# A fused two-block transformer kernel: the slots of the two rings of split weights, 4160 bytes apart in place of 4096

## The chip, the cores and the metric

The kernel runs on one core of a Trainium2 chip. The core has five engines that work side by side: TensorE (PE, matmuls; its weight loads are listed as PEld), VectorE (DVE), ScalarE (ACT), GpSimd (POOL) and SyncE (SP), which here only issues transfers. They share the on-chip memory SBUF, with 128 partitions; matmuls write to the eight banks of PSUM. The metric is the device time of one execution in microseconds, as a median of several runs.

## The reference

The input x is [1, 512, 1024] in float32. A first block applies a mixer (half of its channels by a stabilised mLSTM in chunks, half by gated linear attention, both forward and backward) and a convolutional gated network; a second block of two layers applies a pooling and convolution mixer or a latent attention, cross attention to a memory of 256 rows, and again a gated network. Each part is preceded by an RMS norm. Cut to its frame:

```python
def first_block(x, ...):
    x = x + rms_norm(hybrid_mixer(rms_norm(x, g0), w_in, ..., w_out), g1)
    x = x + rms_norm(conv_ffn(rms_norm(x, g2), w_gate, w_up, conv_w, conv_b, w_down), g3)
    return x

def second_block(x, mem, ...):
    for l in range(2):
        h = rmsnorm(x, norm_mix_g[l])
        x = x + (pool_conv_mixer(h, ...) if l == 0 else mla_attention(h, ...))
        x = x + memory_cross_attention(rmsnorm(x, ...), rmsnorm(mem, ...), wq, wkv, wo)
        x = x + conv_ffn_2(rmsnorm(x, ...), w_up, conv_w, conv_b, w_down)
    return rmsnorm(x, final_norm_g)
```

Nearly all of the arithmetic is products of activations with weight matrices, in float32.

## The kernel before

Activations lie transposed in SBUF: 128 channels on the partitions, 512 positions along a row, eight such tiles for 1024 channels. The weights were laid out in units of 128 partitions by up to 1024 numbers (4096 bytes in each partition). Unit u goes to slot u % 4 (RING is 4) of three rings. SyncE loads it into `raw`. Then it is split into two numbers of a shorter format, high and low: GpSimd writes wH = raw + 0 (L637) and, once that is done, wL = raw - wH (L640). For 40 units (a_o, b_r and the memory's weights) ScalarE writes the high part (L1583) and GpSimd the low part only (L695 and L707). Activations are split in the same way, into hnH and hnL or actH and actL.

TensorE makes each product out of three matmuls (L750 to L752): high by high, low by high and high by low. A ring tile is either the weight operand (128x128 at a time) or the moving one (up to 512 columns). A unit with all 512 positions is 8 x 3 = 24 matmuls of 512 columns. When a unit's last matmul is done, `unit_done` rises; GpSimd waits for it before it writes the slot again, and TensorE waits for `split` before it reads the next unit. SyncE waits for `split` before it loads raw again. The order of all this is written out in the program; nothing in it looks at an address.

The helper `at` gives each tensor the next free address in a partition, rounded up to 64 bytes. By it raw begins at 100544, wH at 116928 and wL at 133312, each ring 16384 bytes long, followed by the vectors VT, the constants CT, MASK, zero, rstd, rcol, ssq, sq, lnb, lncol and onesR, then a reserved gap of 1536 bytes and tmpY. Earlier are XT at 1472, hnH at 17856, hnL at 34240, actH at 50624, actL at 67008 and MIX at 83392. The line numbers of the changed kernel are one higher from L38 on.

The prediction also speaks of L680 (GpSimd, low part of an activation out of MIX and hnH), L736 (GpSimd, MIX by rstd over the last 256 positions), L2263 and L2869 (VectorE, low parts of activations and of the memory's keys and values).

Of the kernel before, what the change touches and what calls it, by code (L numbers as in the profile page):

```python
# [17 lines left out]
F32R = mybir.dt.float32r  # L18
I32 = mybir.dt.int32
ALU = mybir.AluOpType  # L20
ACT = mybir.ActivationFunctionType
AX = mybir.AxisListType

P = 128
# [10 lines left out]
ENDS = (slice(0, 256), slice(256, 512))  # L35
RING = 4
UNIT = 1024
BIG = 1e30  # L38
HALVES = (1, 2, 4, 8, 16, 32, 64)
POOL_WINDOWS = (2, 4, 8, 16)  # L40
# [235 lines left out]
def program(nc, x_t, mem_t, positions, weights, pool_w, gla_w2, vecs, consts, masks, out):  # L276
    ctx = ExitStack()
    with ctx:
        place = [1472]

        def at(name, shape, dt=F32, offset=None):

            size = int(np.prod(shape[1:])) * 4
            if offset is None:
                offset = place[0]
                place[0] += (size + 63) // 64 * 64
            return nc.alloc_sbuf_tensor_at(name, shape, dt, offset=offset)

        def sem(name):
            return ctx.enter_context(nc.semaphore(name))  # L290
# [10 lines left out]
        MIX = at("MIX", [P, KD, S])  # L301
        place[0] += 768
        raw = at("raw", [P, RING, UNIT])
        wH = at("wH", [P, RING, UNIT], F32R)
        wL = at("wL", [P, RING, UNIT], F32R)
        VT = at("VT", [P, NVEC])
        CT = at("CT", [P, NCONST])
        neg_at = place[0]
# [9 lines left out]
        lnb = at("lnb", [P, S])  # L318
        lncol = at("lncol", [P, NB])
        onesR = at("onesR", [P, P], F32R)  # L320
        place[0] += 3 * 512
        tmpY = at("tmpY", [P, 1])
        scr = place[0]
        TOP = 229344
# [146 lines left out]
        def sig(name):  # L471

            if name not in named:
                named[name] = sem(name)
            return named[name]
# [15 lines left out]
        def psum(n):  # L491
            return bank[BANK[n]]
# [1039 lines left out]
        def _(act):  # L1532
            step, nsq = [0], [0]
            run = nc.scalar.activation
# [43 lines left out]
            def memory_high(i):  # L1578

                u = MEMORY[i]  # L1580
                act.wait_ge(loaded[u % RING], 16 * (u // RING + 1))
                act.wait_ge(unit_done, u - RING + 1)
                run(wH[:, u % RING, :], raw[:, u % RING, :], ACT.Copy).then_inc(sig("memory_hi"), 1)  # L1583

            def memory_input(l):

# [131 lines left out]
            for i in range(9):  # L1718
                if i < 8:
                    decay(i)  # L1720
                if i == 0:
                    first_values()
                if 1 <= i <= 4:
                    log_gate(i - 1)
                elif i > 4:
                    if i == 5:
                        first_fade(3)
                    if i == 8:
                        memory_high(0)
                        memory_high(1)  # L1730
                    n = TILE0["b_v"] + i - 5
                    tile_wait(act, n)
                    free(run(VB[:, i - 5, :], psum(n)[:, :], ACT.Copy, scale=rcol[:, i - 5:i - 4]), n)
# [31 lines left out]
            for cc in range(2):  # L1765
                for lev in range(1, 10):
                    if 2 <= lev <= 7:
                        key_mix(cc, lev)
                    if cc == 0 and lev in (4, 6, 8) or (cc, lev) == (1, 2):
                        memory_high(4 + (lev // 2 - 2 if cc == 0 else 3))  # L1770
                    if cc == 0 and lev in (2, 3):
                        memory_high(lev)
                        if lev == 3:
                            act.wait_ge(sig("y_sums"), 8)
                        for h in (2 * lev - 4, 2 * lev - 3):
                            gone_wait(act, TILE0[f"nd{2 * h + 1}"])
                            gone_wait(act, TILE0[f"nd{2 * h + 1}"] + 1)
                            for b in range(NB):
                                run(sq[:, h % 2, b * P:b * P + P], Y[:, b, h, :], ACT.Square, accum_out=ysq[:, 4 * h + b:4 * h + b + 1])\
                                    .then_inc(sig("y_sums"), 1)  # L1780
                    if cc == 0 and lev == 4:
                        act.wait_ge(sig("y_sums"), 16)
                        link(run(yln[:, :], ysq[:, :], ACT.Ln, bias=v("eps"), scale=1.0 / P))
                        link(run(yrt[:, :], yln[:, :], ACT.Exp, scale=-0.5))
                    if cc == 0 and 5 <= lev <= 8:
                        h = lev - 5
                        for b in range(NB):
                            run(Y[:, b, h, :], Y[:, b, h, :], ACT.Copy, scale=yrt[:, 4 * h + b:4 * h + b + 1])\
                                .then_inc(sig("y_scaled"), 1)
                    if cc == 1 and lev in (3, 5, 7, 9):  # L1790
                        h = (lev - 3) // 2
                        act.wait_ge(sig("head_out"), h + 1)
                        run(actH[:, h, :], psum(TILE0["y_turn"] + h)[:, :], ACT.Copy).then_inc(sig("y_hi"), 1)
                    if cc == 1 and lev in (2, 4):
                        head_square(lev // 2 - 1)
# [435 lines left out]
        def _(dve):  # L2231
# [814 lines left out]
            def att_max(h):  # L3046

                for t, b, c0, o in SCORE_AT:
                    n = TILE0["score"] + 3 * h + t
                    if o != 2:  # L3050
                        tile_wait(dve, n)
                    w = (b + 1) * P
                    own = psum(n)[:, c0 * P:c0 * P + w]
                    last = nc.vector.tensor_tensor_reduce(own, own, not_past[:, S - w:], -scale, BIG, ALU.add, ALU.min,
                                                          mst[:, h % 2, o:o + 1])
# [29 lines left out]


# [1 line left out]
def columns(a):  # L3088

# [20 lines left out]
def lay_weights(a):  # L3110
# [38 lines left out]
    for i, (gate, up, down) in enumerate(layers):  # L3149
        pairs = np.stack([stationary(gate), stationary(up)], axis=1).reshape(2 * NF, P, D)  # L3150
        at = 0
        for t, c in enumerate(THIRDS):
            groups[f"ff{i}_gu{t}"] = pairs[2 * at:2 * (at + c)]
            groups[f"ff{i}_d{t}"] = stationary(down[at * P:(at + c) * P])
            at += c
    laid = np.zeros((NUNITS, P, UNIT), np.float32)
    for name, count, width in UNITS:
# [34 lines left out]
def constants():  # L3192
# [4 lines left out]
    def put(name, w):  # L3197
        laid[:, CONST[name]:CONST[name] + w.shape[1]] = w
    put("ident", (p == f) * 1.0)
    put("ones", np.ones((P, P)))  # L3200
    put("past", (f < p) * BIG)
    put("future", (f > p) * BIG)
    put("upto", (p <= f) * 1.0)
    put("since", (p >= f) * 1.0)
    put("twice", (p == f) * 2.0)
    put("neg_future", (f > p) * -BIG)
    counts = [np.minimum(np.arange(16) + 1, w).astype(np.float32) for w in POOL_WINDOWS]
# [28 lines left out]
```

## Time and profile before

| | us |
|---|---|
| median of 3 runs (2006.04 to 2006.3) | 2006.12 |
| the profiled execution | 2006.59 |
| its span in the trace | 2004.8 |
| TensorE busy in it | 1981.7 (99%) |
| GpSimd busy | 1448.1 (72%) |
| VectorE busy | 971.0 (48%) |
| ScalarE busy | 616.6 (31%) |

The span is the time between the first and the last recorded instruction. Matmuls are pipelined: one of 512 columns is recorded as some 390 ns long, while the next starts after 227 ns or so; the starts tell the rate. The granted clock of TensorE was 0.998 of full speed in the mean of the core.

### The profile page before, as it was taken

Reading aid. Unit: us, or ns where it says so; the run is one execution under the profiler, and the core shown is the slowest. Engines: PE = TensorE matmul, PEld = TensorE weight load, DVE = VectorE, ACT = ScalarE, POOL = GpSimd, SP = SyncE. Lnnn points to the kernel's source line nnn. Section 1 sums busy time; section 2 is a strip of 40 time slices with the busy share of each in tenths; the row PEclk is TensorE's granted clock in tenths of the full one; section 3 lists DMA queues with packets and bytes.
Section 4 is the critical chain, followed back from the end, with each engine's and each line's share of the span. In section 5 each row is a group of like instructions: output and inputs, shape, how many; then the busy total and the mean of one; then the engine's idle time right before and its main releaser. Section 6 shows DMA issues by size and latency. Waiting matters only on the chain.

```text
span 2004.8 us, 25752 instructions
## 1 busy us (share of the span) xinstructions
PE 1981.7 (99%) x9476; PEld 1625.3 (81%) x9476; DVE 971.0 (48%) x1607; ACT 616.6 (31%) x1172; POOL 1448.1 (72%) x736
## 2 busy tenths in 40 slices
PE   8999989999999999999999999999999999999998
PEld 6788778888888888888888888877678888888887
DVE  5566444233433899565431332364656554223134
ACT  5454452221013435433210110136743331011012
POOL 7623379777877877974977778687569398777774
PEclk9999999999999999999999999999999999999999
DMA  4741233222323345321332223234013123222322
GB/s 166 145 66 64 76 109 116 94 95 95 96 91 108 106 145 170 109 81 53 109 102 95 94 94 102 72 101 123 2 33 109 49 95 105 95 95 96 102 84 66
DMA packets 58299, 190.79 MB, mean 95 GB/s; under 512 B 6416, under 2 KB 10256, under 8 KB 58096
## 3 DMA queue, kind: packets, MB, share of 16 engines
q1 hardware_dynamic: 54720, 184.42, 29.9%
q10 hardware_dynamic: 3472, 4.88, 0.8%
q8 instruction: 76, 1.25, 0.3%
q14 instruction: 31, 0.25, 0.0%
HBM read 183.50 MB, written 2.10 MB: 93 GB/s over the span
## 4 chain that ended last, share of the span: by engine, by line
PE 96%; POOL 1%; ACT 1%; DVE 1%; DMA 1%; SPq 0%; issue 0%; DVEq 0%; POOLq 0%
PE bank L750 29%; PE bank L751 29%; PE bank L752 29%; PE bank L1458 2%; PE bank L1135 1%; PE bank L1472 1%; PE bank L1488 1%; PE bank L1046 1%; DMA raw<-weights 1%; POOL wL L640 0%; POOL wH L637 0%; PE bank L1208 0%; PE bank L1157 0%; PE bank L990 0%; SPq L585 0%; PE bank L1149 0%
## 5 line engine op out<-in xcount | busy, mean ns | idle before, releaser
L637 POOL TENSOR_TENSOR wH<-raw,zero 128x1024 fp32r<-128x1024 f32 (+1 forms) x303 | 579.5, 1912 | 376.5 <-PE bank L752 358.9
L640 POOL TENSOR_TENSOR wL<-raw,wH 128x1024 fp32r<-128x1024 f32 (+1 forms) x303 | 719.6, 2375 | 23.8
L750 PE MATMUL bank<-hnH,wH 128*128 128x512 f32 (+1 forms) x1456 | 571.5, 392 | 14.4 <-POOL wL L631 8.0
L751 PE MATMUL bank<-hnL,wH 128*128 128x512 f32 (+1 forms) x1456 | 568.5, 390 | 0.0
L752 PE MATMUL bank<-hnH,wL 128*128 128x512 f32 (+1 forms) x1456 | 568.1, 390 | 0.0
L750 PEld LDWEIGHTS bank<-hnH,wH 128*128 128x128 f32 (+1 forms) x1456 | 273.4, 188 | 77.2 <-issue 8.2
L752 PEld LDWEIGHTS bank<-hnH,wL 128*128 128x128 f32 (+1 forms) x1456 | 273.6, 188 | 58.6 <-issue 0.7
L751 PEld LDWEIGHTS bank<-hnL,wH 128*128 128x128 f32 (+1 forms) x1456 | 273.7, 188 | 56.4 <-issue 0.2
L750 PE MATMUL bank<-actH,wH 128*128 128x512 f32 (+1 forms) x802 | 309.4, 386 | 0.0
L752 PE MATMUL bank<-actH,wL 128*128 128x512 f32 (+1 forms) x802 | 308.2, 384 | 0.0
L751 PE MATMUL bank<-actL,wH 128*128 128x512 f32 (+1 forms) x770 | 295.7, 384 | 0.0
L2371 DVE TENSOR_TENSOR bank<-bank,rstd 128x512 f32<-128x512 f32 x66 | 46.1, 699 | 283.1 <-PE bank L752 283.1
L752 PEld LDWEIGHTS bank<-actH,wL 128*128 128x128 f32 x802 | 150.7, 188 | 30.1
L750 PEld LDWEIGHTS bank<-actH,wH 128*128 128x128 f32 x802 | 150.7, 188 | 30.1 <-issue 0.2
L751 PEld LDWEIGHTS bank<-actL,wH 128*128 128x128 f32 x770 | 144.7, 188 | 28.7 <-issue 0.2
L1602 ACT ACTIVATE bank<-gpad,VT 128x512 f32<-128x512 f32 x66 | 51.7, 783 | 345.0 <-DVE gpad L2369 345.0
L1605 ACT ACTIVATE cva<-bank 128x512 f32<-128x512 f32 x66 | 39.5, 599 | 369.1 <-DVE bank L2295 369.1
L707 POOL TENSOR_TENSOR wL<-raw,wH 128x1024 fp32r<-128x1024 f32 x32 | 76.6, 2404 | 30.6 <-ACT wH L1583 30.3
L2398 DVE TENSOR_TENSOR XT<-bank,XT 128x512 f32<-128x512 f32 x32 | 22.1, 692 | 135.3 <-PE bank L752 135.3
L2758 DVE SCALAR_TENSOR_TENSOR bank<-glp,VT,bank 128x512 f32<-128x512 f32 x120 | 81.9, 747 | 0.1
L1553 ACT ACTIVATE hnH<-XT,VT 128x512 fp32r<-128x512 f32 x48 | 34.6, 721 | 131.2 <-DVE XT L2845 106.4
L2369 DVE TENSOR_TENSOR gpad<-bank,rstd 128x512 f32<-128x512 f32 x66 | 45.7, 692 | 56.9 <-PE bank L752 56.8
(418 smaller groups left out, 2580.1 us busy)
## 6 DMA issues: line engine op xcount, KB each, us to landing
raw<-weights SPq DMA_DIRECT2D x315, 512.0 KB, 3.5
raw<-weights SPq DMA_DIRECT2D x28, 384.0 KB, 3.0
XT<-x_t SPq DMA_DIRECT2D x8, 256.0 KB, 6.5
XT<-x_t ACTq DMA_DIRECT2D x1, 2048.0 KB, 8.5
maxB<-rowM SPq DMA_DIRECT2D x7, 256.0 KB, 16.6
out<-MIX SPq DMA_DIRECT2D x13, 128.0 KB, 1.9
qkO<-qkA SPq DMA_DIRECT2D x4, 256.0 KB, 4.1
memT<-mem_t ACTq DMA_DIRECT2D x1, 1024.0 KB, 5.4
```

The lines of the kernel that those rows point to most:

```text
L637: nc.gpsimd.tensor_tensor(wH[:, slot, 0:w], raw[:, slot, 0:w], nothing.broadcast_to([P, w]), ALU.add)\
L640: nc.gpsimd.tensor_tensor(wL[:, slot, 0:w], raw[:, slot, 0:w], wH[:, slot, 0:w].bitcast(F32), ALU.subtract).then_inc(split, 1)
L707: nc.gpsimd.tensor_tensor(wL[:, slot, 0:w], raw[:, slot, 0:w], wH[:, slot, 0:w].bitcast(F32), ALU.subtract).then_inc(split, 1)
L750: mm(out_, aH, bH, start=first, stop=False)
L751: mm(out_, aH, bL, start=False, stop=False)
L752: return mm(out_, aL, bH, start=False, stop=last)
L1458: last = mm(psum(n)[:, c0 * P:c0 * P + w], QC[0:96, h, b * P:b * P + P], KC[0:96, h, 0:w], start=True, stop=True)
L1602: run(psum(n)[:, :], gpad[:, s_, mid:mid + S], ACT.Identity, bias=v(f"fconv_b{f}", q), scale=v(f"fconv_w{f}", 3 * q + 1)).then_inc(sig("co ...
L1605: free(run(cva[:, s_, :], psum(n)[:, :], ACT.Gelu_apprx_tanh if f == 0 else ACT.Silu), n)
L2369: tt(gpad[:, s_, 2:2 + S], psum(n)[:, :], rstd[:, :], ALU.mult).then_inc(sig("gate_in"), 1)
L2371: tt(psum(n + 1)[:, :], psum(n + 1)[:, :], rstd[:, :], ALU.mult)
L2758: ins = stt(psum(n)[:, :], glp[:, c_, k:k + S], w, psum(n)[:, :], ALU.mult, ALU.add)
```

## The change

The two rings wH and wL get slots of 1040 numbers (4160 bytes), of which the first 1024 are used as before. Each ring becomes 256 bytes longer. The reserved gap behind onesR becomes 512 bytes shorter, so that all that lies behind it keeps its address; what lies between wL and the gap moves by 512 bytes, and wL itself by 256. The ring raw keeps its slots of 4096 bytes. ScalarE's high part, which wrote a whole slot, now names the first 1024 numbers of it. No instruction is added, taken away or moved on any engine, and none has another shape.

```diff
 RING = 4
 UNIT = 1024
+SLOT = UNIT + 16
...
         raw = at("raw", [P, RING, UNIT])
-        wH = at("wH", [P, RING, UNIT], F32R)
-        wL = at("wL", [P, RING, UNIT], F32R)
+        wH = at("wH", [P, RING, SLOT], F32R)
+        wL = at("wL", [P, RING, SLOT], F32R)
...
         onesR = at("onesR", [P, P], F32R)
-        place[0] += 3 * 512
+        place[0] += 1024
         tmpY = at("tmpY", [P, 1])
...
-                run(wH[:, u % RING, :], raw[:, u % RING, :], ACT.Copy).then_inc(sig("memory_hi"), 1)
+                run(wH[:, u % RING, 0:UNIT], raw[:, u % RING, :], ACT.Copy).then_inc(sig("memory_hi"), 1)
```

## Rows read from the trace of the kernel before

**Rows 1.** The page, part 1: busy us (share of the span) xinstructions.

```profile
PE 1981.7 (99%) x9476; PEld 1625.3 (81%) x9476; DVE 971.0 (48%) x1607; ACT 616.6 (31%) x1172; POOL 1448.1 (72%) x736
```

**Rows 2.** The page, part 4: the chain that ended last, by engine.

```profile
PE 96%; POOL 1%; ACT 1%; DVE 1%; DMA 1%; SPq 0%; issue 0%; DVEq 0%; POOLq 0%
```

**Rows 3.** Timeline of 1099 to 1108 us: start us, us, engine line op [idle before].

```profile
1099.32 1.90 POOL L637 TENSOR_TENSOR wH<-raw,zero 128x1024 fp32r<-128x1024 f32 x1 [1.07 <-PE bank L752]
...
1099.66 0.39 PE L750 MATMUL bank<-hnH,wH 128*128 128x512 f32 x1
...
1104.66 1.89 POOL L637 TENSOR_TENSOR wH<-raw,zero 128x1024 fp32r<-128x1024 f32 x1 [0.98 <-PE bank L752]
...
1107.82 0.39 PE L750 MATMUL bank<-hnH,wH 128*128 128x512 f32 x1
```

**Rows 4.** Busy time by stretch: us, then each engine's, granted clock, DMA share, GB/s.

```profile
1000.00:1200.00 200.00, 200.00 (x884) 165.62 (x883) 62.82 (x90) 25.76 (x39) 154.78 (x74) 1.00 0.29 95
```

**Rows 5.** Waits of PE: engine line waited for, us in total, times, longest.

```profile
PE bank L750 <- POOL wL L631: 8.0, 1, 8.0
PE bank L750 <- DVE hnL L2263: 5.6, 1, 5.6
...
PE bank L750 <- POOL wL L640: 0.7, 3, 0.3
```

**Rows 6.** The chain in order of time, 0 to 75 us: start us, us, what.

```profile
13.54 1.90 POOL wH L637
...
15.51 2.42 POOL wL L640
...
57.53 2.72 POOL wL L640
60.25 2.30 POOL wH L637
...
66.96 2.37 POOL wL L640
```

**Rows 7.** Groups of POOL by form: line engine op names shapes xcount, busy, mean ns.

```profile
L640 POOL TENSOR_TENSOR wL<-raw,wH 128x1024 fp32r<-128x1024 f32 x275 | 667.5, 2427 | 21.6
L637 POOL TENSOR_TENSOR wH<-raw,zero 128x1024 fp32r<-128x1024 f32 x275 | 537.4, 1954 | 335.2 <-PE bank L752 317.6 <-DMA raw<-weights 17.4
...
L680 POOL TENSOR_TENSOR hnL<-MIX,hnH 128x512 fp32r<-128x512 f32 x4 | 5.2, 1294 | 9.4 <-ACT XT L1871 9.4
L736 POOL TENSOR_TENSOR MIX<-MIX,rstd 128x256 f32<-128x256 f32 x2 | 1.4, 726 | 14.8 <-ACT rstd L2224 14.8
```

**Rows 8.** Timeline of POOL, 1310 to 1352 us.

```profile
1325.64 2.73 POOL L640 TENSOR_TENSOR wL<-raw,wH 128x1024 fp32r<-128x1024 f32 x1
1335.73 1.89 POOL L637 TENSOR_TENSOR wH<-raw,zero 128x1024 fp32r<-128x1024 f32 x1 [7.36 <-PE bank L752]
...
1344.40 2.34 POOL L637 TENSOR_TENSOR wH<-raw,zero 128x1024 fp32r<-128x1024 f32 x1
```

**Rows 9.** The page, part 5: the first and last of the six largest matmul groups.

```profile
L750 PE MATMUL bank<-hnH,wH 128*128 128x512 f32 (+1 forms) x1456 | 571.5, 392 | 14.4 <-POOL wL L631 8.0
...
L751 PE MATMUL bank<-actL,wH 128*128 128x512 f32 (+1 forms) x770 | 295.7, 384 | 0.0
```

**Rows 10.** Timelines of PE near 777 and near 872 us (matmuls of 256 columns).

```profile
777.22 0.28 PE L750 MATMUL bank<-memH,wH 128*128 128x256 f32 x1
...
777.94 0.28 PE L750 MATMUL bank<-memH,wH 128*128 128x256 f32 x1
...
871.51 0.28 PE L751 MATMUL bank<-KL,qH 128*128 128x256 f32 x1
...
872.23 0.28 PE L751 MATMUL bank<-KL,qH 128*128 128x256 f32 x1
```

**Rows 11.** The line L2869: duration ns min/median/max, first and last start us.

```profile
L2869 DVE TENSOR_TENSOR VL<-VM,actH x8: 680/1878/1978, 880.2 to 1583.5; 128x512 fp32r<-128x512 f32 x8
```

**Rows 12.** Busy time by stretch, behind PE's idle time at 274 us.

```profile
280.20:286.90 6.70, 6.63 (x19) 5.30 (x20) 6.35 (x11) 5.29 (x11) 2.58 (x2) 0.64 0.23 78
```

## The prediction

> **What bounds the kernel now.** I read the page's busy times first: the reader is to see TensorE (PE) busy in 1981.7 of 2004.8 us, 99%, against 72% for GpSimd (POOL) and less for the others [rows 1]. Only a change that makes PE's work shorter, or that keeps PE waiting, can be seen in the time. The chain that ended last says the same by engine, 96% PE, 1% each for POOL, ACT, DVE and DMA [rows 2]. So there are two places where an address in the rings could matter: the rate at which PE reads the split weights, and the POOL passes that write them, where those stand on the chain.
>
> PE's rate is read from the timeline in a steady stretch of the gated network. From the start at 1099.66 to the start at 1107.82 lie 36 matmuls of 128x512, so one starts each 8.16/36 = 0.2267 us [rows 3]. In 1000 to 1200 us there are 884 matmuls in 200 us, 0.2262 us each, with PE busy in all of it [rows 4]; meanwhile POOL was busy for 155 us with reading and writing the rings. A clash between POOL and PE that came and went with POOL's passes would spread these starts; the average leaves no room for it. At 2.4 GHz, the granted clock of the stretch (1.00), 512 columns are 213.3 ns, so 13.3 ns are added to each.
>
> Where PE waited for POOL is in the list of waits: 8.0 us once, at the first unit, and 0.7 us in three later waits [rows 5]. POOL stands on the chain in 13.5 to 17.9 us and in 55.6 to 69.3 us, which is one pair of passes (high part L637, low part L640) and then three more, four pairs in all [rows 6]. Elsewhere a pair costs 1.90 + 2.43 us [rows 3, 7], its high parts start 5.34 us apart (1099.32 and 1104.66), and PE needs 24 x 0.2267 = 5.44 us for a unit [rows 3]: POOL has about 1 us to spare per unit and waits for PE.
>
> **The change part by part.** The instructions are the same, in the same order on every engine, with the same shapes; only addresses differ.
>
> 1. The slots of wH and wL go from 4096 to 4160 bytes apart, and wL starts 256 bytes later. Before, slot s of raw, wH and wL lie exactly 16384 bytes apart, so a pass reads and writes at the same position modulo 4096 (the allocations in the code: 100544, 116928, 133312). After, raw and wH of slot s differ by 64 s more, raw and wL by 256 + 64 s more. What POOL pays for equal positions is read by comparison. Two inputs of 128x256: L736 reads MIX and rstd, whose addresses are 2880 and 832 bytes apart modulo 4096 (c_ = 0 and 1), and takes 726 ns. The two-input pass over equal positions, 128x512 at L680 (MIX is 65536 bytes behind hnH), takes 1294 ns, and 128x1024 at L640 2427 ns [rows 7]. If position cost nothing these must lie on one line: 726 + (2427 - 726)/3 = 1293 ns. They do. So the step is priced at 0 ns per pass. Bounds, below: L640 gets as quick as L637, which reads one full tensor and a broadcast column, 2427 - 1954 = 473 ns less, four times on the chain, -1.9 us. Above: the slowest usual forms of both passes in this trace, 2.73 us for L640 and 2.34 us for L637 [rows 8], against some 2.40 (2.37 and 2.42 in rows 6) and 1.89. On the chain that is 0.33 us on three L640 (the one at 57.53 is at 2.72 already) and 0.45 us on three L637 (the one at 60.25 is at 2.30 already): 1.0 + 1.35 = +2.3 us. I take 0, since the comparison is of the same kind of instruction.
>
> The Trainium skill's GPSIMD Engine Reference, section 2.1, says that the two inputs of such a pass share one physical read port and cannot do better than about 2.5 cycles an element. An estimate from that page at its 1.2 GHz is 2.13 us for 1024 elements; if the present 2.43 us fell to it, four passes would give back 1.2 us. Nothing in that rule depends on the address, and by it too the time stays within what can be told apart.
>
> 2. PE reads wH and wL as weights and as moving operand at new addresses. The page's six largest matmul groups on them are 3 x 1456 + 2 x 802 + 770 = 6742 instructions [rows 9], so 0.6 ns on each would be 4.0 us, 0.2%. Do the 13.3 ns come from the rings' addresses? The comparison is at 256 columns (106.7 ns at 2.4 GHz). Cross attention's matmuls on KL, qH, actH and actL, none in a ring, start 6 in 0.72 us (871.51 to 872.23), 120 ns each; those of the memory values, whose moving operand is in the rings, 6 in 0.72 us (777.22 to 777.94), 120 ns as well [rows 10]. Both have 13.3 ns added. So the addition belongs to the matmul, not the ring, and I take 0. Below, the bound would be all 13.3 ns; the matmuls without a ring exclude it as well as they can. Above, no slower spacing at full clock is tied to an address by any row, and 0 is the nearest.
>
> 3. ScalarE's high parts of 40 units (a_o, b_r and the memory's weights) write a slot cut to UNIT. It is the same 128x1024; nothing is added.
>
> 4. The tables and small tensors between wL and tmpY (VT, CT, MASK, rstd, ssq, sq, lnb, onesR) move by 512 bytes; a reserved gap shrinks by as much, so tmpY and all behind it stay. These are read by DVE and ACT. DVE's two-input subtraction shows what sets its time: VL<-VM,actH takes 680 ns at the least and 1878 in the median [rows 11]. Its two inputs always start a multiple of 1024 bytes apart, with other multiples in the first layer than in the second; the instances near 1.9 us are those beside a POOL pass. Cost 0, unless POOL's phase changes: should POOL's passes shift, DVE's long instances shift with them. PE's largest wait on DVE is 5.6 us, at hnL [rows 5], and there the input is a PSUM bank; a shift has little to bite on.
>
> The Trainium skill's page SBUF — State Buffer, section "Who interferes with whom", has one rule, that only the port pair of VectorE and GpSimd is contended and PE and ACT never wait on anyone. The long DVE instances agree. By that rule a new spacing can neither slow nor speed PE, and the sum is the same 0.
>
> Sum: the profiled execution took 2006.59 us, 2004.8 of span and 1.8 around it; with 0 from all four steps it would be the same again. It stands 0.47 us above the runs' median of 2006.12, and against that median the forecast is 2006.1.
>
> **The rivals.**
> A. Equal positions do cost POOL its second read, and the spacing frees it. For it: L640 is 473 ns longer than L637. Against: the straight line through the three two-input passes. Time: -1.9, 2004.2 us. That is still within 0.2%, because only four pairs are on the chain.
>
> B. PE's 13.3 ns come, in part or whole, from where the weights lie relative to the moving tensors. For it: they are 6% of nearly every matmul. Against: the same 13.3 ns without a ring. In whole, 6742 x 13.3 ns = 90 us, about 1916; a twentieth of it is 4.5 us, about 2001.6. This is the only way to a clear gain.
>
> C. Slower: odd multiples of 64 bytes cost POOL, and its passes take 2.34 and 2.73 us everywhere. A pair, 5.07 us, plus 0.08 us between passes is still under PE's 5.44, so the steady stretches hide it. It would show where POOL was just in time: the +2.3 us on the chain, and, if PE takes the last of them at once, the three pairs that POOL runs without a break from 1335.73 to about 1349 us [rows 8]: 3 x 0.33 + 2 x 0.45 = +1.9. Together +4.2, 2010.3 us. It decides from a pair about 0.75 us longer; from 1 us longer POOL would be the bound in the steady stretches too. Against: the same straight line, with one operand pair that is not at equal positions.
>
> D. The spacing doesn't act at all, because nothing depends on the position of the slots. That is my forecast, and its sign in the trace is equality of every group.
>
> A fifth matter is the clock: at 280.2 to 286.9 us the granted mean is 0.64 after PE's idle time at 274 to 280, and 19 matmuls take 6.7 us where 19 x 0.2267 = 4.3 would do, a cost of 2.4 us [rows 12]. As no instruction before it changes its duration, I expect it again at the same place; without it the time would be 2.4 us less, 2003.7, just under the range.
>
> **How the numbers follow.** Forecast (D) 0.82, at 2006.1; A 0.06, at 2004.2; B 0.06, of it 0.01 inside 0.2%; C 0.05, all slower; 0.01 is left to matters unnamed and counted as no change. A difference under about 0.2%, 4 us, can't be told from no change. Faster is thus 0.05, slower 0.05, same 0.90. The range takes in the low bound of step 1 (2004.2) and its high bound on the chain (2008.4): 2004.0 to 2008.5.
>
> **What would show it.** Right: means of 2427 ns for L640 and 1954 for L637, the usual L637 at 1.89; 0.2267 us between matmul starts near 1100 us; PE's waits for POOL 8.0 and 0.7 us again; the clock low once, near 280 us. Rival A shows as L640 nearer 1950, B as a spacing below 0.226 or above 0.228, C as L637 near 2.34 us everywhere and PE waiting for POOL beyond 3 us. The forecast is wrong if the time moves by over 4 us, and its reasoning is wrong if a pass or the spacing moves by over 2% even with the time unmoved.

## The result and the profile after

The changed kernel takes 2031.88 us, a median of 4 runs (2030.73 to 2032.16), against 2006.21 us of 4 runs before: a ratio of 1.0125, with a 95% interval of 1.0112 to 1.0137. It is 25.7 us slower. The forecast was no change, with 2008.5 us as the top of the range.

Busy times, the changed kernel's page (part 1), against [rows 1]:

```profile
PE 2007.4 (99%) x9476; PEld 1627.2 (80%) x9476; DVE 978.2 (48%) x1607; ACT 616.2 (30%) x1172; POOL 1449.2 (71%) x736
```

PE is busy 25.7 us longer, the whole loss, with the same 9476 matmuls. DVE grew by 7.2 us and POOL by 1.1 us; ACT fell by 0.4 us. The chain by engine, against [rows 2], has PE at 98% and POOL at 0%:

```profile
PE 98%; ACT 1%; DVE 1%; DMA 0%; SPq 0%; POOL 0%; issue 0%; DVEq 0%; ACTq 0%
```

So PE waits for nobody more than before, which its waits say too (engine, line waited for, us in total, times, longest), against [rows 5]:

```profile
PE bank L751 <- POOL wL L632: 7.5, 1, 7.5
PE bank L751 <- DVE hnL L2264: 5.8, 2, 5.6
...
PE bank L751 <- POOL wL L641: 0.5, 2, 0.3
```

The two GpSimd passes, by form, take 2438 and 1944 ns where [rows 7] had 2427 and 1954:

```profile
L641 POOL TENSOR_TENSOR wL<-raw,wH 128x1024 fp32r<-128x1024 f32 x275 | 670.6, 2438 | 21.6
L638 POOL TENSOR_TENSOR wH<-raw,zero 128x1024 fp32r<-128x1024 f32 x275 | 534.6, 1944 | 355.9 <-PE bank L753 338.5 <-DMA raw<-weights 17.4
```

What changed is the rate of the matmuls. The stretch of [rows 4] holds 870 of them in place of 884, PE again busy in all of it:

```profile
1000.00:1200.00 200.00, 200.00 (x870) 163.16 (x869) 64.47 (x93) 28.29 (x43) 156.55 (x73) 1.00 0.29 96
```

That is 0.2299 us each in place of 0.2262, at the same granted clock of 1.00. (Such a count also takes in the matmuls that the edges of the stretch cut, so it is a little low; the starts are exact.) Over the matmuls of 512 columns that read a ring and are followed by the next start within 300 ns (7361 of 7462), the mean from one start to the next is 230.5 ns, and 227.0 ns before: 3.5 ns x 7361 = 25.8 us.

Which matmuls pay shows when the units are told apart. A unit's slot is known by counting GpSimd's low passes (the m-th fills slot m % 4). In the changed kernel's timeline of PE these are the first matmuls of four units in a row, in slots 0, 1, 2 and 3, and of the next in slot 0:

```profile
1123.50 0.39 PE L751 MATMUL bank<-hnH,wH 128*128 128x512 f32 x1
...
1128.95 0.40 PE L751 MATMUL bank<-hnH,wH 128*128 128x512 f32 x1
...
1134.55 0.39 PE L751 MATMUL bank<-hnH,wH 128*128 128x512 f32 x1
...
1140.12 0.39 PE L751 MATMUL bank<-hnH,wH 128*128 128x512 f32 x1
...
1145.63 0.39 PE L751 MATMUL bank<-hnH,wH 128*128 128x512 f32 x1
```

The 24 matmuls take 5.45 us in slot 0, 5.60 in slot 1, 5.57 in slot 2 and 5.51 in slot 3. Before, each took 5.44. Slot 0 of wH has the address it had, and slot 0 of wL lies 256 bytes later: this costs next to nothing. The slots that lie 64, 128 and 192 bytes further do cost. That POOL's passes were not behind it shows already here: matmuls that start while POOL, DVE and ACT are all idle are 230.5 ns apart as well (some 900 of them).

### The profile page after: what moved, and what is told of

Its sections match the earlier page's. It is cut to its first block, busy times and chain, and to the rows that moved or that the text cites. A ratio compares the mean times of both kernels' runs of the same rounds, so it can differ in the third digit from the quotient of the medians.

```text
span 2030.0 us, 25752 instructions
## 1 busy us (share of the span) xinstructions
PE 2007.4 (99%) x9476; PEld 1627.2 (80%) x9476; DVE 978.2 (48%) x1607; ACT 616.2 (30%) x1172; POOL 1449.2 (71%) x736
## 4 chain that ended last, share of the span: by engine, by line
PE 98%; ACT 1%; DVE 1%; DMA 0%; SPq 0%; POOL 0%; issue 0%; DVEq 0%; ACTq 0%
PE bank L751 30%; PE bank L753 30%; PE bank L752 30%; PE bank L1459 2%; PE bank L1136 1%; PE bank L1473 1%; PE bank L1489 1%; PE bank L1047 1%; DMA raw<-weights 0%; PE bank L1209 0%; PE bank L1158 0%; PE bank L991 0%; SPq L586 0%; PE bank L1150 0%; PE bank L1101 0%; PE bank L1270 0%
```

## The experiments

The theory, R: before, all that PE reads together with a ring slot (hnH, hnL, actH, actL, and behind tmpY the tiles memH, memL, cH, cL and poolL) begins at the same address modulo 256 as every slot, at 192. A matmul is slowed when its weights and its moving operand differ there. The rivals: G, GpSimd's passes at unequal positions clash with PE's reads; A, the absolute address of a weight block counts; S, the spacing of 4096 itself helps; T, the moved tables cost. Experiments 1 to 11 ran once each, experiment 12 ten times, with the kernel before beside them on the same chip: 2007.59 us for experiments 1 to 4 and 2006.13 for 5 to 8, one run each, and a median of 2006.54 over 13 runs for 9 to 12. Those 13 lie between 2005.71 and 2007.82 us, so a single run tells differences of more than about 2 us.

The numbers on slots below are the mean ns from one start to the next in units whose 24 matmuls read hnH, hnL and the rings, in slots 0 to 3 (30 to 38 units each); the last column is the mean over all ring matmuls of 512 columns, taken as above:

| kernel | rings against hn, modulo 256, by slot | slot 0 | 1 | 2 | 3 | all ring matmuls |
|---|---|---|---|---|---|---|
| before | 0 | 226.7 | 226.7 | 226.7 | 226.7 | 227.0 |
| after | 0, 64, 128, 192 | 227.1 | 233.2 | 232.3 | 229.6 | 230.5 |
| 1, tables only | 0 | 226.7 | 226.7 | 226.7 | 226.7 | 227.0 |
| 2, 4352 apart | 0 | 226.7 | 226.7 | 226.7 | 226.7 | 227.0 |
| 3, rings +64 | 64 | 233.3 | 233.3 | 233.3 | 233.3 | 233.1 |
| 4, whole map +64 | 0 | 226.7 | 226.7 | 226.7 | 226.7 | 227.0 |
| 5, activations +64 | 192 | 229.0 | 228.9 | 228.9 | 228.9 | 229.4 |
| 6, 4224 apart | 0, 128, 0, 128 | 227.3 | 232.9 | 227.4 | 232.9 | 230.4 |
| 7, wH alone | wH 0, 64, 128, 192; wL 0 | 227.1 | 233.2 | 232.9 | 230.6 | 230.8 |
| 8, wL alone | wL 0, 64, 128, 192; wH 0 | 226.8 | 230.9 | 231.9 | 231.1 | 230.2 |
| 9, rings +128 | 128 | 233.1 | 233.1 | 233.1 | 233.1 | 232.9 |
| 10, rings +32 | 32 | 233.3 | 233.3 | 233.3 | 233.3 | 233.3 |
| 11, raw -64 | 0 | 226.7 | 226.7 | 226.7 | 226.7 | 227.0 |

**1. The spacing undone, the rest kept.**

```diff
         wH = at("wH", [P, RING, UNIT], F32R)
+        place[0] += 256
         wL = at("wL", [P, RING, UNIT], F32R)
+        place[0] += 256
...
-        place[0] += 3 * 512
+        place[0] += 1024
```

> Slots 4096 apart again; only what came with the spacing stays: wL starts 256 bytes later, VT, CT, rstd and the other small tensors 512 bytes later. Theory R (the matmul's two reads, the running moving operand and the weight load of the next matmul, cost more when their addresses differ modulo 256; in the trace after, ring matmuls start 227.1 ns apart in slot 0, 232 to 233 in slots 1 and 2, 229.5 in slot 3): every address modulo 256 is that of before, so 226.7 ns everywhere and about 2006.2 us. Theory T (the moved tables and wL's base cost the time): about 2032 us.

2007.36 us: T falls. wL's base and the tables' new places cost nothing.

**2. Another spacing that is a multiple of 256.** The edit is one of the changed kernel:

```diff
-SLOT = UNIT + 16
+SLOT = UNIT + 64
...
-        place[0] += 768
+        place[0] += 256
         raw = at("raw", [P, RING, UNIT])
         wH = at("wH", [P, RING, SLOT], F32R)
...
         onesR = at("onesR", [P, P], F32R)
-        place[0] += 1024
```

> Slots of wH and wL 4352 bytes apart, 4096 + 256 (raw begins 512 bytes earlier to make room). Theory R: a multiple of 256, so all slots at 226.7 ns and about 2006.2 us. Theory S (a spacing that is a multiple of 4096 is what helps, any other costs): 2030 us or more. Theory G (GpSimd's passes clash with PE's reads when raw and the rings are not at the same position modulo 4096): about 2030 us.

2007.46 us, and the steady stretch is that of before:

```profile
1000.00:1200.00 200.00, 200.00 (x884) 165.67 (x883) 63.10 (x91) 26.35 (x40) 154.75 (x73) 1.00 0.29 95
```

S falls, and so does G in the form that I gave it: slots at unequal positions modulo 4096 are free as long as they are equal modulo 256.

**3. The old spacing, both rings 64 bytes later.**

```diff
         raw = at("raw", [P, RING, UNIT])
+        place[0] += 64
         wH = at("wH", [P, RING, UNIT], F32R)
         wL = at("wL", [P, RING, UNIT], F32R)
...
         onesR = at("onesR", [P, P], F32R)
-        place[0] += 3 * 512
+        place[0] += 3 * 512 - 64
```

> Slots 4096 apart, but both rings begin 64 bytes later (wH and wL and the small tensors behind them), so that every slot is at the position that slot 1 of wH and wL has after the change (modulo 256). Theory R: every slot like slot 1 there, about 5.7 ns on each of some 7370 ring matmuls of 512 columns, +42 us, 2048 us, spacing near 232.4 ns in all slots. Theory A (the absolute address of the weight block modulo 256 is what counts): the same. Theory S (the spacing is the cause): 2006 us.

2050.34 us, 42.8 above its kernel before: nearly the number of R, with slots 4096 apart. The steady stretch has 859 matmuls:

```profile
1000.00:1200.00 200.00, 200.00 (x859) 161.15 (x858) 64.72 (x93) 27.75 (x42) 155.13 (x73) 1.00 0.30 95
```

The same trace shows a sign that R did not foresee. Matmuls of 256 columns get quicker with their weights 64 bytes above. These two starts in the memory's keys, with the ring as weights, have 42 matmuls from the one to the other:

```profile
791.55 0.28 PE L751 MATMUL bank<-memH,wH 128*128 128x256 f32 x1
...
796.32 0.28 PE L751 MATMUL bank<-memH,wH 128*128 128x256 f32 x1
```

4.77 us are 113.6 ns each, where the same product took 120 in the kernel before [rows 10].

**4. The whole map 64 bytes later.**

```diff
-        place = [1472]
+        place = [1536]
```

> Slots 4096 apart and the whole map of SBUF 64 bytes later, activations and rings alike. Theory R (only the difference of the two addresses counts): 226.7 ns and 2006.2 us. Theory A (the absolute address of the weight block, or of any operand, modulo 256 counts): near 232 ns and 2048 us.

2005.43 us and 884 matmuls: A falls. The weights have the absolute addresses of experiment 3, but the activations moved along, and the loss is gone.

```profile
1000.00:1200.00 200.00, 200.00 (x884) 165.62 (x883) 62.11 (x89) 25.76 (x39) 155.40 (x73) 1.00 0.29 95
```

**5. The activations moved and the rings left.**

```diff
+        place[0] += 64
         hn_at = place[0]
...
-        place[0] += 768
+        place[0] += 704
```

> Slots 4096 apart and the rings where they were; hnH, hnL, actH, actL and MIX begin 64 bytes later instead. Against the activations the rings are 64 bytes earlier, modulo 256 the same as 192 later, the difference of slot 3 after the change. Theory R: every ring matmul on hn or act like slot 3 there, about 2.8 ns on each, some +20 us, 2026 us. Theory A (absolute address of the weight block): 2006 us where the rings are the weights.

2023.67 us, 17.5 above its kernel before. A ring tile that did not move is slowed, to 229 ns, like slot 3 after the change; A would have none of that. The steady stretch:

```profile
1000.00:1200.00 200.00, 200.00 (x876) 164.17 (x875) 64.09 (x92) 27.70 (x42) 154.75 (x72) 1.00 0.30 98
```

Experiments 3 and 5 have a second reading, in a product where the roles are turned: near 60 us the rings are the moving operand and hn is the weights. Now experiment 3 has weights minus moving at -64, and experiment 5 at +64. The timeline of PE in experiment 3, two starts with 42 matmuls from the one to the other (14 triples):

```profile
57.12 0.39 PE L752 MATMUL bank<-wL,hnH 128*128 128x512 f32 x1
...
66.73 0.39 PE L752 MATMUL bank<-wL,hnH 128*128 128x512 f32 x1
```

and in experiment 5:

```profile
56.80 0.40 PE L752 MATMUL bank<-wL,hnH 128*128 128x512 f32 x1
...
66.60 0.39 PE L752 MATMUL bank<-wL,hnH 128*128 128x512 f32 x1
```

9.61 us are 228.8 ns each, and 9.80 us are 233.3. (A row names the moving operand first, then the weights.) The costs have changed places with the roles: 233 ns belongs to weights 64 bytes above the moving operand, 229 to 64 below, whichever of the two tensors was moved. This is what R needs and no rival gives.

Nor is a ring needed. In cross attention, PXH and PXL are moving operands that stay in place in experiment 5, while their weights (actH and VL) begin 64 bytes later. From one start to the other there are 6 matmuls in the kernel before:

```profile
889.99 0.39 PE L750 MATMUL bank<-PXH,actH 128*128 128x512 f32 x1
...
891.35 0.39 PE L750 MATMUL bank<-hnH,wH 128*128 128x512 f32 x1
```

and 9 in experiment 5:

```profile
896.98 0.39 PE L751 MATMUL bank<-PXH,actH 128*128 128x512 f32 x1
...
899.08 0.40 PE L751 MATMUL bank<-hnH,wH 128*128 128x512 f32 x1
```

1.36 us are 226.7 ns each, and 2.10 us are 233.3. The products with qH have 256 columns and no ring either, and there the sign is the other one again. In experiment 5 qH, the weights of two matmuls in three, lies 64 bytes below actH and KL modulo 256, and the 24 matmuls from 878.74 to 881.56 us start 117.5 ns apart in place of 120.

**6. 4224 apart.** SLOT = UNIT + 32 in the changed kernel, with a gap of 512 bytes.

```diff
-SLOT = UNIT + 16
+SLOT = UNIT + 32
...
-        place[0] += 1024
+        place[0] += 512
```

> Slots 4224 bytes apart, 4096 + 128: slot offsets 0, 128, 256, 384. Theory R with a period of 256: slots 0 and 2 near 227 ns, slots 1 and 3 like slot 2 after the change (232.3 ns), in the mean 2.8 ns on 7370 matmuls, +20 us, 2027 us. If the period were 512, slot 2 would cost as well: over 2035 us.

2030.25 us, 24.1 above its kernel before, where I had 20. The pattern is right, slots 0 and 2 nearly free (227.3 and 227.4 ns) and 1 and 3 at 233, so slot 2 at 256 bytes is as good as 0. The cost was put a little low: 2.8 ns in the mean over all ring matmuls, where 230.4 - 227.0 = 3.4 were measured.

**7 and 8. One ring alone.** In the changed kernel, 7 gives wL back its old form (256 bytes of padding behind it), 8 wH (the same):

```diff
-        wL = at("wL", [P, RING, SLOT], F32R)
+        wL = at("wL", [P, RING, UNIT], F32R)
+        place[0] += 256
```

> Only wH has slots of 4160 bytes; wL keeps 4096. Theory R, with a cost for each matmul by the pair of reads it makes: two of three weight loads are from wH, so two thirds of the change's 25.7 us, +17 us, 2023 us. If the cost sits in the jump between wH and wL (their positions equal or not), it is about the whole: 2032 us or more.

> Only wL has slots of 4160 bytes; wH keeps 4096. Theory R, by the pair: one of three weight loads is from wL, so one third of the change's 25.7 us, +9 us, 2015 us. If the cost sits in wH and wL being at different positions, about the same as with only wH.

2033.25 and 2029.98 us, +27.1 and +23.9 us, in place of +17 and +9. Both forecasts of R missed: its price by the matmul is wrong. The cost does not add up by matmuls: one ring out of place costs about as much as two, though of three matmuls only two (or one) have weights there. Perhaps a slowed read holds up the ones behind it as well; that is not shown. In slot 1 the mean from a matmul's start to the next, in the order hnH by wH, hnL by wH, hnH by wL, is 236, 229 and 235 ns with wH alone, and 228, 229 and 236 with wL alone. Neither "the matmul with the misplaced weights" nor "the one during whose run they are loaded" gives both rows.

The second reading in both expectations, a cost of the jump between wH and wL, came out in both: "about the whole", and "about the same". It can't be the cause of the change's loss, for after the change, as in experiments 3, 9 and 10, wH and wL lie at equal positions modulo 256 and the loss is there. Whether such a jump adds something in 7 and 8 is not shown.

**9 and 10. Other distances.** The edit of 3 with 128, and with 32 (and 32 more behind wL).

```diff
+        place[0] += 32
         wH = at("wH", [P, RING, UNIT], F32R)
         wL = at("wL", [P, RING, UNIT], F32R)
+        place[0] += 32
...
         onesR = at("onesR", [P, P], F32R)
-        place[0] += 3 * 512
+        place[0] += 3 * 512 - 64
```

> Slots 4096 apart, both rings begin 128 bytes later. Theory R (weights minus moving operand, modulo 256, sets a matmul's spacing): all slots like slot 2 after the change, 232.3 to 232.9 ns in place of 226.7, so 7370 x 5.9 ns = +43 us, 2049 us. A theory that only an odd multiple of 64 costs would give 2006 us.

> Slots 4096 apart, both rings begin 32 bytes later. How fine is it? If the cost comes with a 64-byte step alone (both addresses in the same 64-byte piece are alike), 2006 us; if any difference modulo 256 costs, between 2020 and 2050 us. Theory R leaves both open; I hold the second for likelier.

2051.14 and 2050.74 us. 32 bytes cost as much as 64 or 128. In the steady stretch of experiment 10:

```profile
1000.00:1200.00 200.00, 200.00 (x859) 161.15 (x858) 64.87 (x93) 27.72 (x43) 155.38 (x73) 1.00 0.29 95
```

**11. raw alone.**

```diff
-        place[0] += 768
+        place[0] += 704
         raw = at("raw", [P, RING, UNIT])
+        place[0] += 64
         wH = at("wH", [P, RING, UNIT], F32R)
```

> Only raw, which PE never reads, begins 64 bytes earlier; wH, wL and all else stay. GpSimd's two passes then read and write at different positions, as after the change. Theory R: no change, 2006 us with matmuls 226.7 ns apart and the low pass at 2.43 us. Theory G (GpSimd's passes at unequal positions clash with PE's reads): some +25 us, 2032 us.

2005.40 us: G falls altogether. GpSimd's passes by form, at unequal positions also modulo 256, are those of [rows 7] within 1 ns:

```profile
L641 POOL TENSOR_TENSOR wL<-raw,wH 128x1024 fp32r<-128x1024 f32 x275 | 667.7, 2428 | 21.6
L638 POOL TENSOR_TENSOR wH<-raw,zero 128x1024 fp32r<-128x1024 f32 x275 | 537.0, 1953 | 334.5 <-PE bank L753 317.3 <-DMA raw<-weights 16.8
```

**12. The fourth kernel again, in ten runs.** The edit of 4.

> The kernel of the fourth experiment again, the whole map 64 bytes later, timed. That one was 2.2 us under its kernel before in a single look (2005.4 against 2007.6), all of it in the first 12 us. Theory R: same as before within 0.1%, ratio 1.000. A rival (absolute addresses are worth 2 us): ratio 0.999 with an interval clear of 1.

2006.00 us, 10 runs, ratio 0.9999 (0.9989 to 1.0009). The 2.2 us between the two single runs of experiment 4 were a difference of runs. No kernel tried is faster than the kernel before by more than runs differ.

## Why the prediction was wrong

**Step 1, GpSimd's passes: right.** They moved by +11 and -10 ns, 0.5%, and by under 1 ns with raw alone out of place. The straight line through three pass lengths was a fair comparison, since one of its pairs did lie at another position, modulo 4096 and modulo 256.

**Step 2, PE's reads: the step that failed.** It priced the new addresses at 0 ns for each of the ring matmuls; they cost 3.5 ns in the mean, 25.7 us in all. The comparison behind the 0 was empty. I set ring matmuls of 256 columns beside matmuls without a ring [rows 10] and found 120 ns in both. But KL, qH, actH and actL start at the same address modulo 256 as the rings of before (1472, the start of the map, and all that follows it there in steps of 256). Two rows with equal positions can't tell what unequal ones cost. I had worked out the addresses for GpSimd's pass and did not do it for PE's operands. The rows at 777 us were also misread: they are the memory's keys, with the ring as weights and memH as the moving operand, not the values. Nor could rows of 256 columns have given the price at 512: with the weights 64 bytes above, matmuls of 256 columns get quicker (113.6 ns in place of 120 in experiment 3) and those of 512 slower (233.3 in place of 226.7).

The second fault is in the bound. Step 2 should have been bounded on both sides. Below it got 13.3 ns; above I wrote that no row tied a slower spacing to an address, and took 0 as the end. That no row shows it is the reason for a bound, not against one. 0.6 ns per matmul was already written down as the 4 us that decide, and a bound of the same size as the one below, +13.3 ns, would have put the range at up to 90 us on that side. Rival B was accordingly allowed in one direction only. It named the true cause, where the weights lie relative to the moving operand, but at 512 columns, nearly all of the kernel, the sign is the other one: no distance tried went below 226.7 ns, and so no run ties the 13.3 ns there to addresses. At 256 columns part of them does go with the distance. The steady 226.7 ns, from which I had argued against a clash between POOL and PE, came from a map in which the addresses of both operands agree.

The rule from the Trainium skill's page SBUF — State Buffer, section "Who interferes with whom", is about ports shared by two engines. It also calls PE's own two read ports, one for the moving operand and one for the weights, independent. I drew from it that a new spacing can't slow PE. That PE waits for no other engine agrees with the traces, as the loss shows with the other engines idle too. But the rate does depend on how PE's own two operands lie to each other, and there the measurement decides.

**Steps 3 and 4: right.** Experiment 2 keeps ScalarE's cut slot and costs nothing, at 2007.46 against 2007.59 us. Experiment 1 has the moved tables and wL's base alone, at 2007.36. The long two-input operations of DVE had no part in it.

**The rivals.** A and C concerned GpSimd's passes and did not come about. C was the only slower case in the sum, with all of the 0.05 for slower, and from the wrong engine. D, no effect, fell. The clock fell once, near 282 us, about as before: 12 starts in a row came 0.43 us apart there, in place of 9. By an estimate from these rows, 3 x (0.43 - 0.23), that is 0.6 us of the difference.

## What to carry to other kernels

Work out the address modulo 256 of the weights and the moving operand of every frequent matmul before moving or padding a buffer. In this kernel those of 512 columns started 226.7 ns apart at equal residues and 229 to 233 ns at others, 1% to 2% of a kernel that is bound by PE. Where such matmuls prevail, pad in multiples of 256 bytes, or move all operands together. Matmuls of 256 columns behaved the other way (120 ns at equal residues, 114 to 118 with the weights 64 bytes above), so measure the shape that counts. And a comparison only bears on an address if the rows compared differ in it, while a cost that no row shows needs an upper bound as much as a lower one.

## What was not expected of the hardware

- A matmul with 512 columns and its weight load (both in the split format) takes 226.67 ns at full clock when the two operands agree modulo 256, and 233.3 ns when the weights lie 32 or 64 bytes above: 544 and 560 cycles at 2.4 GHz. With the weights 64 bytes below (the same as 192 above) it is about 229. At 128 it is 233.1 in the mean with single starts from 228 to 241 ns apart.
- With 256 columns it is 120 ns at equal residues, 288 cycles at 2.4 GHz, and 113.6 in the quickest stretch with the weights 64 bytes above (experiment 3), about 273 cycles.
- Offsets of 256, 512 and 768 bytes between slots are free (experiment 2), and so is a common shift of all operands by 64 (experiments 4 and 12).
- One third of the weight loads out of place (wL alone) costs nearly as much as all: 23.9 us against 25.7.

What stays open: which of the two reads holds up the other, and at which point; the rows of experiments 7 and 8 contradict both simple accounts. Why the sign turns between 256 and 512 columns is open too. Distances under 32 bytes were not tried. Of plain float32 matmuls, experiment 5 changes one pair of operands (P, 256 columns, against VB), from 128 bytes apart to 64, and they start 216 ns apart in both kernels; equal residues and other shapes were not compared.
